# Transposes of the mixing steps by way of DRAM and VectorE, and steps that open with the scores

## The reference, cut to what matters

```python
h = rms_norm(x, norm_mix[l])
proj = jnp.einsum('bsd,de->bse', h, w_in[l])
q_a, k_a, v_a, u_b, q_c, k_c, v_c, g_c = jnp.split(proj, IN_SPLITS, axis=-1)
# A: window attention, 8 query heads on 2 key heads, 64 wide, keys of this chunk and the one before
q, k = rms_norm(q, q_gain), rms_norm(k, k_gain)
sc = einsum('bnqhgd,bnkhd->bnhgqk', qb, kb) * HEAD_DIM ** -0.5
p = softmax(concatenate([sc, sink], -1), -1)[..., :-1]
o = einsum('bnhgqk,bnkhd->bnqhgd', p, vb)
# B: causal means over 2/4/8/16 frames, a small map per group
# C: retention, 4 heads: q, k = rope(q), rope(k); inner products with decay, plus a carried state
mix = jnp.concatenate([y_a, y_b, y_c], axis=-1)
x = x + jnp.einsum('bse,ed->bsd', mix, w_out[l])
x = x + moe_ffn(rms_norm(x, norm_ffn[l]), ...)        # shared router, group-limited top-2
```

## Time and profile before

| | |
|---|---|
| runs, median | 3064.96 us |
| the profiled execution | 3065.28 us, span 3063.4 us, mean granted clock of TensorE 0.998 |
| a mixing stage | about 800 us of a layer; a factored step is 46.2 us |
| PE busy | 3020.4 us (99%) |
| DVE, ACT, POOL busy | 46%, 20%, 34% |

### The profile page before, as it was taken

One profiled execution on the slowest core, in us unless ns is written; L12 is line 12 of the kernel. 1 busy time (PEld: TensorE's weight loads), 2 busy tenths in 40 slices (PEclk: granted clock), 3 DMA queues, 4 the chain that ended last, 5 costly groups with the idle time before them and its releaser, 6 DMA issues.

```text
span 3063.4 us, 53173 instructions
## 1 busy us (share of the span) xinstructions
PE 3020.4 (99%) x18160; PEld 2156.8 (70%) x18160; DVE 1402.9 (46%) x3996; ACT 616.8 (20%) x1930; POOL 1041.3 (34%) x1250
## 2 busy tenths in 40 slices
PE   9999999999999999999999999999999999999998
PEld 4555555555799999888845555555557999998887
DVE  5576677667322222211155776776673222221211
ACT  2222322323111111101123223223221111111101
POOL 1132132133255555423112232232232555553322
PEclk9999999999999999999999999999999999999999
DMA  8656656653689999999965656657536999999996
GB/s 325 248 198 231 240 191 240 240 183 127 252 291 318 310 320 350 341 355 345 331 252 206 212 204 249 213 203 250 197 131 240 303 303 315 346 335 352 350 351 221
DMA packets 248448, 816.95 MB, mean 267 GB/s; under 512 B 68304, under 2 KB 120528, under 8 KB 189264
## 3 DMA queue, kind: packets, MB, share of 16 engines
q1 hardware_dynamic: 201344, 733.80, 64.6%
q0 software_dynamic: 46112, 77.70, 10.9%
q10 hardware_dynamic: 720, 2.00, 0.2%
HBM read 718.95 MB, written 95.56 MB: 266 GB/s over the span
## 4 chain that ended last, share of the span: by engine, by line
PE 91%; DVE 3%; DMA 2%; issue 1%; DVEq 1%; SPq 1%; ACT 0%; POOL 0%; ACTq 0%; POOLq 0%
PE bank L2120 31%; PE bank L1822 19%; PE bank L1887 13%; PE bank L2160 9%; PE bank L2150 6%; PE bank L1793 5%; PE bank L1721 2%; PE bank L1974 1%; PE bank L2015 1%; PE bank L2049 1%; DMA out<-arena 1%; PE bank L1898 1%; DMA arena<-out 0%; PE bank L1983 0%; DVE arena L1238 0%
## 5 line engine op out<-in xcount | busy, mean ns | idle before, releaser
L2120 PEld LDWEIGHTS bank<-arena,wts 128*128 128x128 f32 x8192 | 983.8, 191 | 17.7 <-issue 17.7
L2120 PE MATMUL bank<-arena,wts 128*128 128x128 f32 (+7 forms) x8192 | 988.0, 283 | 3.5 <-issue 2.1
L1822 PE MATMUL bank<-wts 128*128 128x512 f32 x1056 | 469.5, 596 | 0.0
L1887 PE MATMUL bank<-wts,arena 128*128 128x512 f32 x1024 | 455.4, 597 | 1.5 <-ACT arena L1064 1.5
L1696 DVE TENSOR_TENSOR arena<-arena,bank 128x128 f32<-128x128 f32 (+6 forms) x64 | 19.1, 299 | 902.8 <-ACT arena L1130 902.8
L1822 PEld LDWEIGHTS bank<-wts 128*128 128x128 f32 x1056 | 195.0, 190 | 219.7 <-issue 218.1
L836 POOL DMA_INDIRECT arena<-hrows,arena x288 | 287.3, 998 | 167.7 <-issue 153.5
L1887 PEld LDWEIGHTS bank<-wts,arena 128*128 128x128 f32 x1024 | 190.1, 191 | 216.8 <-issue 214.8
L732 POOL TENSOR_TENSOR arena<-arena 128x256 f32<-128x256 f32 x32 | 25.4, 795 | 851.7 <-DVEq L1432 851.7
L862 POOL DMA_INDIRECT out<-arena x176 | 275.1, 1563 | 54.6 <-issue 52.1
L2160 PE MATMUL bank<-arena,wts 128*128 128x135 f32 (+6 forms) x2176 | 280.1, 289 | 0.0
(11 more groups left out here) (274 smaller groups left out, 3117.1 us busy)
## 6 DMA issues: line engine op xcount, KB each, us to landing
wts<-in_w_gate SPq DMA_DIRECT2D x128, 1024.0 KB, 8.3
wts<-in_w_up SPq DMA_DIRECT2D x128, 1024.0 KB, 10.9
wts<-in_w_down SPq DMA_DIRECT2D x128, 1024.0 KB, 17.3
wts<-wt SPq DMA_DIRECT2D x96, 1024.0 KB, 5.9
wts<-in_w_in SPq DMA_DIRECT2D x88, 1024.0 KB, 7.1
hrows<-arena SPq DMA_DIRECT2D x36, 512.0 KB, 5.4
out<-arena SPq DMA_DIRECT2D x36, 512.0 KB, 3.2
wt<-arena SPq DMA_DIRECT2D x16, 1024.0 KB, 4.4
```

The costliest lines, as they stand in the source:

```text
L1822: i = mm(bIP[j in (1, 3, 6)][:, :], own[:, d], ring[k % SLOTS][:, d], start=(d == 0 and j in (0, 1, 3)), stop=(d == 3), skip_group_check=True)
L1887: i = mm(bIP[k][:, :], dT[o][:, d - 4] if d in (4, 5) else mixT[:, d], wout[:, d, 512 * k:512 * k + 512], start=(n == 0), stop=(n == DC - 1))
L2120: return mm(gu_at(f, k, w), lhs, xT[:, d, 0:w], start=start, stop=(d == DC - 1), skip_group_check=True)
```

## The change

- q, k and the rotated rows of tiles 0 to 14 are no longer transposed by PE. DVE (`qk_scaled`) and POOL write them in a blocked order into one tile `qkr` of 1280 columns; ACT stores it to DRAM and reads it back in four pieces (`qkr_out`, `qkr_back`) at the end of a step; DVE transposes it (`qkr_turn`) ahead of `add_x`. POOL writes the rotated k once more in token order, for the state.
- The probabilities of steps 1 to 14 go the same way: ACT stores them behind the exponentials, reads them back in four pieces behind the router's parts, DVE transposes them behind `z_ready`. Tile 15 and step 15 keep PE's transposes.
- PE opens a step with the scores; the exponentials stand behind the eviction of factor 0.
- DVE opens a step with the mask and maxima (`largest`), then `norm_2` in late steps, `add_blocks` in even steps, `finish_columns(s, 0)`, `softmax`, `h2T_in`, and only then `qk_sums`.
- The gains of q and k are multiplied into one factor on k. SP's program has no edit.

The diff, cut to its core:

```diff
@@ ACT, step
+                    def qkr_out():
+                        wait_alone(e, qk_ready, t0 + 1)
+                        wait_alone(e, rope_ready, t0 + 1)
+                        e.dma_start(qkr_rows[b], qkr).then_inc(qkr_stored, 16)
+                    def qkr_back():
+                        wait_alone(e, qkr_stored, (l * (TILES - 1) + s + 1) * 16)
+                        for k in range(4):
+                            e.dma_start(qkr_pieces[32 * k:32 * k + 32, :]..., qkr_rows[b][...]).then_inc(qkr_in, 16)
...
                     if s in FACTORED:
                         partial_columns(s, 0)
-                        partial_columns(s, 1)
...
+                    if back:
+                        exponentials()
+                        e.drain()
                         if s + 3 < TILES:
                             sumsq_front(s + 3)
+                        if s < TILES - 1:
+                            wait_alone(e, probs_ready, t0)
+                            e.dma_start(probs_rows[o], pr_flat).then_inc(probs_stored, 16)
+                    if s in FACTORED:
+                        partial_columns(s, 1)
...
                     if tail and s != TILES:
                         router_in()
+                    if back and s < TILES - 1:
+                        wait_alone(e, probs_stored, (l * (TILES - 2) + s) * 16)
+                        for k in range(4):
+                            e.dma_start(pr_flat[32 * k:32 * k + 32, :]..., probs_rows[o][...]).then_inc(probs_in, 16)
...
                         a(mixT[:, 6:8]..., bE[:, 0:256], ACT.Copy, scale=0.5).then_inc(ycT_ready, 1)
+                        if s < TILES - 1:
+                            qkr_out()
+                            qkr_back()
@@ DVE
+                def qkr_turn(t):
+                    r = t % 2
+                    e.wait_ge(qkr_in, (l * (TILES - 1) + t + 1) * 64)
+                    for c in range(2):
+                        v.transpose(kTr[:, :, c, r]..., of_token[:, 2 * c:2 * c + 2, 4:6])
+                    for c in range(2):
+                        v.transpose(qT[:, c]..., of_token[:, 2 * c:2 * c + 2, 0:4])
+                    e.drain()
+                    v.tensor_scalar(kTr[:, :, :, r], kTr[:, :, :, r], qgs[:, 0:1], None, ALU.mult)
+                    v.transpose(rT..., of_token[:, :, 6:10])
+                    e.drain().then_inc(qkr_turned, 1)
...
-                    if front and back:
-                        qk_sums(s)
-                    if s in FACTORED:
-                        finish_columns(s, 0)
...
+                    if back and s < TILES:
+                        largest()
+                        if s >= LATE:
+                            norm_2(s - 1)
+                        if s % 2 == 0 and s < 13:
+                            add_blocks(s - 1)
+                        if s in FACTORED:
+                            finish_columns(s, 0)
+                        softmax()
+                        if tail:
+                            h2T_in()
+                    if front and back:
+                        qk_sums(s)
...
+                    if back and s < TILES - 1:
+                        e.wait_ge(probs_in, (l * (TILES - 2) + s) * 64)
+                        v.transpose(prT..., pr_flat)
+                        e.drain().then_inc(pT_ready, 1)
...
                     if back and s < TILES - 1:
+                            qkr_turn(s)
                         add_x(s, o, 0)
                         add_x(s, o, 1)
-                        if s % 2 and s < 12:
-                            add_blocks(s)
-                        if s + 1 >= LATE:
-                            norm_2(s)
@@ PE
+                    def scores():
+                        banks_free()
+                        e.wait_ge(qkr_turned, l * (TILES - 1) + s)
...
+                    if back and s < TILES:
+                        scores()
                     fill(0)
                     fill(1)
-                    if back:
-                        e.wait_ge(qkT_ready, t0)
...
-                    if back:
+                    if back and s >= TILES - 1:
                         e.wait_ge(probs_ready, t0)
```

More of the change, by code:

```diff
@@ L49 @@
 PAD_STORES = 2 * (PADS // P) + 2
+ITEMS = 10
+QKR = 4 * 32 * ITEMS
 EPS = 1e-6
@@ L172, in program @@
     wt = nc.dram_tensor("wt", (8 * P, 2048), F32).ap()
+    probs_rows = [nc.dram_tensor(f"probs_rows{b}", (P, D), F32).ap() for b in range(2)]
+    qkr_rows = [nc.dram_tensor(f"qkr_rows{b}", (P, QKR), F32).ap() for b in range(2)]
     hpieces, opieces = (t.rearrange("t (a c) -> (t a) c", a=4) for t in (hrows, out))
@@ L747, in step @@
                         e.drain()
-                        e.tensor_tensor(dst[:, :, 0], rtmp[:, 0], rtmp[:, 1], ALU.subtract)
-                        e.tensor_tensor(dst[:, :, 1], rtmp[:, 2], rtmp[:, 3], ALU.add)
+                        for k, op in enumerate((ALU.subtract, ALU.add)):
+                            if s == TILES - 1:
+                                e.tensor_tensor(rk_last.rearrange("p (h k d) -> p h k d", h=8, k=2)[:, :, k], rtmp[:, 2 * k], rtmp[:, 2 * k + 1], op)
+                                continue
+                            for a in range(2):
+                                one, two = (rtmp[:, 2 * k + n].rearrange("p (j a) d -> p j a d", a=2)[:, :, a] for n in range(2))
+                                e.tensor_tensor(by_item[:, a, 6:10, k], one, two, op)
+                            e.tensor_tensor(own[:, :, k], rtmp[:, 2 * k, 4:8], rtmp[:, 2 * k + 1, 4:8], op)
                         e.drain().then_inc(rope_ready, 1)
@@ L1052, in step @@
                     if back:
-                        e.wait_ge(pe_pT, t0)
-                        for k in range(2):
-                            a(prT[:, k].rearrange("p g n -> p (g n)"), (bC, bD)[k][:, :], ACT.Copy)
-                        e.drain().then_inc(pT_ready, 1)
+                        if s >= TILES - 1:
+                            e.wait_ge(pe_pT, l * 2 + s - TILES + 2)
+                            for k in range(2):
+                                a(prT[:, k].rearrange("p g n -> p (g n)"), (bC, bD)[k][:, :], ACT.Copy)
+                            e.drain().then_inc(pT_ready, 1)
                         if s == TILES:
@@ L1350, in step @@
                             make(i)
+                        e.wait_ge(made_stored[1], (l + 1) * 48)
+                        qkr_turn(0)
                         hT_of(3)
@@ L1383, in step, with softmax @@
                         e.drain().then_inc(neg_max, 1)
-                    if tail and s != TILES:
-                        if back:
-                            h2T_in()
-                        else:
-                            norm_2(TILES)
-                            e.wait_ge(pe_numbers, l + 1)
-                            spot(0)
-                    if s == TILES:
-                        add_x(TILES - 1, b, 1)
-                    if back:
+                    def softmax():
                         e.wait_ge(tanh_gate, t0)
@@ L1912, in step, with banks_free @@
                         e.wait_ge(act_out, whole_out(l, TILES - 1, 3))
-                    if back:
-                        if first:
-                            e.wait_ge(uT_ready, t0)
+                    def banks_free():
                         if not first:
@@ L1938, in fold @@
                         i.then_inc(pe_fold, 1)
+                    def scores():
+                        if first:
+                            e.wait_ge(uT_ready, t0)
+                        if s == TILES:
+                            e.wait_ge(last_turned, l + 1)
+                        else:
+                            banks_free()
+                            e.wait_ge(qkr_turned, l * (TILES - 1) + s)
+                        for g in range(2):
+                            for c in range(2):
+                                for a in range(2):
+                                    ph = slice(64 * a, 64 * a + 64)
+                                    q = qT[ph, c, g].rearrange("p j n -> p (j n)")
+                                    at = (2 * g + c) * P
+                                    dst = (bC, bD)[a]
+                                    if c == 0:
+                                        f = kTr[ph, g].rearrange("p c r n -> p (c r) n")
+                                        keys = f[:, o:4 - o:3 - 2 * o]
+                                    else:
+                                        keys = kTr[ph, g, :, o]
+                                    mm(dst[:, at:at + P].rearrange("p (c n) -> p c n", c=2), q, keys, start=True, stop=True)
+                        if not first:
+                            e.wait_ge(attn_ready, t0 - 1)
+                            e.wait_ge(z_ready, t0 - 1)
+                        for j in range(2):
+                            for a in range(2):
+                                ph = slice(64 * a, 64 * a + 64)
```

(8 more changed lines are left out.)

150 lines of the change are left out of this document (89 added, 61 removed).

## The result

The changed kernel takes 3315.04 us (median of 4 runs, 3308.74 to 3320.63) against 3065.69 us (3063.11 to 3068.70) for the kernel before in the same series: ratio 1.0812, 95% interval [1.0790, 1.0834]. It is slower by 249 us; the forecast was 3246, range 3145 to 3350.

What follows compares the result with a forecast made beforehand. The prediction took PE, busy 99% of the span, as the bound. On a base near 3065 us, 24 x (-1.97 + 7.1 + 2.0) = +171 in factored steps and +10 elsewhere gave 3246 us, range 3145 to 3350.

Steps and rivals of the forecast that it cites:

- The sixth block behind h2n_ready: Factored steps: h2n_ready moves from offset 6.8 to 19.2, so block 5 is issued at 21.7, when PE wants it.
- Landing 7.1, PE waits 7.1: Factor 5 of each factored step: block 5 lands 7.1 us after issue, PE waits that long; ends 4.6 and 10.6.
- The clock, 2.0 us a step: PE in factored steps: the idle wait drops its clock, costing 2.0 us a step; ends 0 and 4.0.
- The step in sum: Each of 24 factored steps: -1.97 for transposes, +7.1 wait, +2.0 clock, together 7.13 us.
- The probabilities by way of DRAM: Products with v in a step: no cost while block 5 is late, -0 to +1 us if it is not.
- +2.4: Step 14: z late, then the DRAM chain, put at +2.4 us.
- The other steps, +10: Steps outside the factored ones, both layers: +10 us in sum, between -10 and +30.
- the estimate for step 1: Step 1: PE wants a bank that ACT evicts late; +4 us in layer 0, less in layer 1, less 2 of transposes.
- q, k and rotated rows through DRAM, taken as 0: End of a step: the chain takes 12.1 to 14.1 of 14.2 us, just fits; +0 to +1.5, taken as 0.
- DVE alone would hold a step at about 47.0: DVE in factored steps: its longer row alone would make a step about 47.0 us if PE did not wait.
- The fourth rival, all hidden, 3008: Whole kernel: the transposes' 57 us go, nothing is late, 3008 up to 3050, if h2n_ready comes before about 12; chance 0.07.

Runs made afterwards that it cites:

- Experiment 2: Kernel before, with SP waiting in factored steps until factor 4 is done before hrows, rot, x and later block loads: 3268.09 us, ratio 1.0661.
- experiment 7: Changed kernel with the transposes of the probabilities given back to PE, SP's order unchanged: 3255.34 us, ratio 1.0618.
- experiment 1: Changed kernel with SP loading blocks 5 to 7 ahead of its wait for h2n_ready, hrows, rot and x: 3328.47 us, ratio 1.0857.
- experiment 6: Changed kernel with SP loading blocks 5 to 7 ahead of h2n_ready and PE transposing the probabilities again: 3062.54 us, ratio 0.9991.
- experiment 11: Kernel of experiment 5 with only half of each factored-step weight block loaded from the fifth block on: 3892.33 us, total not comparable; period 45.3 us.
- experiment 5: Changed kernel with SP loading blocks 5 to 7 before h2n_ready and ACT reading the probabilities before evicting factor 4: 3152.04 us, ratio 1.0276.
- experiment 10: Kernel of experiment 9 with POOL rotating q and k ahead of the product with the gate: 3086.82 us, ratio 1.0073.
- experiment 9: Kernel of experiment 6 with step 1 reordered: two half products before the scores, tile 2's banks evicted around the exponentials: 3053.93 us, ratio 0.9968.
- experiment 3: Changed kernel with 28 small products that nobody reads ahead of factor 5 on PE in each factored step: 3303.52 us, ratio 1.0786.

## Why the prediction was right, and where not

- *The sixth block behind h2n_ready* (most of the forecast): right, in place and order. h2n's row ends at offset 18.8 (19.2 predicted), hrows goes out at 18.9, block 5 at 20.7 (21.7). Experiment 2 shows that it costs 203 us by itself, and experiment 7, which has it without the probabilities' trip, took 3255 us, where the forecast's terms would give 3246 + 28 x 0.88 = 3271.
- *Landing 7.1, PE waits 7.1*: mis-sized. The landing is 8.8 in the step shown and the wait 8.4 in the mean: 24 x 1.3 = +31 us. The missing part is the reads on ACT's queue, which I had kept as an end of the range: without them the landing is 6.9 in the step shown and the wait 5.9 in the mean (experiment 7). My 7.1 was the median of the 88 loads of this group before; in the kernel after the median of the same group is 13.8. The Trainium skill's rule that the prediction weighed (DMA: Bandwidth & Descriptors, Issuing engines are not separate DMA queues) is what the trace shows.
- *The clock, 2.0 us a step*: right. From 436.43 to the next row at 441.93 it is 5.50 us for eight records, where it is 3.49 in the earlier trace rows: 2.0 us lost, behind 7.66 us of idleness. The granted clock is 0.50, the lower level (1.2 GHz), from 436.43 to 440.4, and 0.98 and more behind that. One of the two samples that I took the size from was misread, though: at the kernel's start, from 9.86 to 26.14, the granted clock is 1.00, so no row shows that the 2.3 us lost there were the clock's. The other one (768.79, clock 0.52) stands.
- *The step in sum*: -1.97 + 8.4 + 2.0 = 8.4, measured 54.85 - 46.19 = 8.66 (7.13 predicted); a part of what is left is waits at the scores, 0.6 to 1.7 us in three of the twelve steps. Over 24 steps, with 8.78 in layer 1, that is 209 of the 250 us.
- *The probabilities by way of DRAM cost "nothing while block 5 is late, and -0 to +1 if it is not"*: this step failed. I added a landing of 3.2 and one of 2.8 us from the earlier trace rows; the reads take 7.6 us in the median and 13 us and more to the last piece. Uncovered they cost 10 to 11 us of a step, the clock's fall among them (experiment 1: 54.3 us in the step shown and a period of 55.6 with the blocks in time, where 44.2 was left). Covered they cost 31 us in all (experiment 7), and in step 14 +10 us where I had +2.4 (47.63 against 37.39).
- *The other steps, +10*: measured 250 - 209 = +41, of them +20 in step 14 of both layers, +11 in step 1, +7 in step 15, +5 in the opening of layer 0 and -3 elsewhere. Without the probabilities' trip they are +12 (experiment 7: 191 us in the span, 178 of them in the factored steps), with +1 in step 14 and +4 in step 1. So the estimate for step 1 was fair, and the 29 us between are the step above.
- *q, k and rotated rows through DRAM, taken as 0*: nearly right. With the rest put right most steps run at 45.09 us, and four of twelve wait, 2.1 us at most (experiment 6).
- *DVE alone would hold a step at about 47.0*: right in kind, 1.7 us too high. In experiment 11, where no transfer is late, DVE's row holds the steps at 45.3, 1.1 us above the 44.2 that PE needs. The forecast did not hang on it.
- *The fourth rival, all hidden, 3008*: its condition was h2n_ready before offset 12. Experiment 1 shows that this would not have been enough; there was no such case.

So the time was held because the largest term was right. The two misses, +31 for the landing and +31 for the other steps, have in the main one root: the landings of block 5 and of the probabilities were taken from rows of transfers that stood elsewhere in the step.

## What to carry to other kernels

When a load's issue stands behind a wait in a DMA queue's program, a reorder on a quite different engine can make it late; so list for each moved signal what is queued behind its waiter. Price a new transfer by the landings of transfers issued in the same microseconds of the step, not by the median of its size. And where one late arrival is found, look for the next that it hides before promising its removal: here taking the first away alone made the kernel slower, and taking both gave back 163 of 249 us.

## What the runs showed of the hardware

- Two queues slow each other: four reads of 128 KB on ACT's queue lengthen a 1 MB landing on SP's from 6.9 to 8.8 us (one step each of experiment 7 and of the kernel after; the waits for it are 5.9 and 8.4 us in the mean), and halving SP's blocks shortens those reads from 7.8 to 4.7 us (experiment 11). In the stretch of a step of experiment 5 where they meet (440 to 462) the DMA engines were busy all the time (share 1.00) and moved 349 GB/s, against 0.62 and 221 GB/s over the factored steps of before.
- Small operations of DVE with two inputs (8 columns) take 0.17 us alone and 0.61 to 0.64 beside POOL's elementwise work (experiment 10, 433.53 to 436.71). The product y * y of the inverse root has a mean of 178 ns in experiment 9 and 253 in 10, where POOL runs beside part of them. The Trainium skill (Advanced Engine Details and Errata, Miscellaneous Facts) says that Pool shares a read and a write interface with DVE and conflicts with DVE instructions of two SBUF inputs; this operation is one, so the trace agrees.
- Products that nobody reads can keep the clock from falling, but 28 of them were enough in seven of layer 0's twelve factored steps and not in the other five (experiment 3).
